# Giving the activations of each large stage an address residue modulo 256 bytes of their own

## The chip, the cores and the metric

The kernel runs as one program on one core of one Trainium2 chip. The metric is the device time of an execution in microseconds, as the median of several runs. Lower is better.

## The reference, cut to what matters

The reference is two stacks of two layers over 256 tokens of 1024 features, all float32. Each layer of the first stack projects the tokens, runs three attentions (latent, differential, memory), mixes them through gates, adds a residual with a layer norm, and runs an MLP of width 4096. Each layer of the second stack projects the tokens to 14,912 columns, runs three scans, mixes them through gates, and runs a gated feed-forward of width 2816.

```python
# first stack, a layer (first_block), cut
x = _layernorm(ALPHA * x + merged @ w_out[l], ln1_g[l], ln1_b[l])
f = jnp.square(jax.nn.relu(x @ mlp_w1[l])) @ mlp_w2[l]
x = _layernorm(ALPHA * x + f, ln2_g[l], ln2_b[l])
...
# second stack, a layer (second_block), cut
u = _rmsnorm(h, norm_mix_g[l])
... = _split(u @ w_in[l], IN_SIZES_2)          # three branches and their gates
h = h + merged @ w_out[l]
u = _rmsnorm(h, norm_ffn_g[l])
up = _dwconv(u @ w_up[l], ffn_conv_w[l], ffn_conv_b[l])
h = h + (jax.nn.silu(a_half) * v_half) @ w_down[l]
```

## The kernel before

**Matrix products.** Weights stream from HBM in 768 panels of 128 partitions x 1024 words. A panel lands in a ring of five (`wring`); ScalarE rounds it to float32r (`whi`), VectorE subtracts to get the rest (`wlo`), in rings of four. Activations are kept in the same two parts in one buffer, a `Pair`: chunks of 256 words, first all high parts, then all low parts 8,192 bytes further on (for the usual 8 chunks). A product is three matmuls: high x high, high x low, low x high.

There are two forms. `features` (built by `projB`) holds the weights (128x128) and moves the activations (128x256): a panel is 2 column halves x 4 chunks x 3 = 24 matmuls. `tokens` (built by `projA`) holds the activations (128x128) and moves the weights (128x512): a panel is 2 token halves x 2 chunks x 3 = 12 matmuls. Both are recorded at line 112, so groups are told apart by their tiles: `ps<-uT,whi` is a `features` matmul on uT, `ps<-whi,uT` a `tokens` one.

**Order.** The schedule is a static list. `weave` interleaves generators with weights, so that panels of a projection fill TensorE between the small matmuls of an attention or scan. Every wait is on a named event; no wait is derived from an address.

**Memory.** `Arena` hands out words of each partition, first fit or at a given place (`at=`), and takes a hole back only five panels after it was freed. It starts at byte 82,496, which is 64 modulo 256. `whi` and `wlo` start at bytes 36,992 and 53,376, both 128 modulo 256, and so does each of their 128x128 blocks. Sizes and places are such that every Pair starts at residue 64 except uT, which lies at word 27,168: byte 191,168, residue 192. The parts inside a Pair are multiples of 256 bytes apart, so each chunk has the residue of its Pair.

**The stages that the change touches**, with the Pair of each:

- first stack, projections of layer 0 and of layer 1: xT, with 34 `features` panels and 24 `tokens` panels per layer; nearly all are woven with attention;
- first stack, MLP of each layer: xT (second one), 32 `features` panels, and hid, 4 times 8 `tokens` panels, in long unbroken runs;
- second stack, projections of each layer ("mix"): uT, 109 `features` and 24 `tokens` panels, woven with the scans in large part; the two scan outputs are written into the same buffer (`uT.again`) for their branch products;
- second stack, up-projection of each layer ("ffn"): uT again, 44 `features` panels without a break.

Pairs that stay as they are, at residue 64: memT, cq, ckv, oM, oD, oE, merged, ym, the 22-chunk hid of the second stack, pT, hT.

Of the kernel before, what the change touches and what calls it, by code (L numbers as in the profile page):

```python
# [9 lines left out]
F32R = mybir.dt.float32r  # L10
# [6 lines left out]
DEPTH = 2  # L17
# [39 lines left out]
class Signals:  # L57
# [5 lines left out]
    def __init__(self, nc, ctx):  # L63
        self.nc, self.ctx = nc, ctx
        self.sems, self.count, self.value, self.sure = {}, {}, {}, False
# [91 lines left out]
class Buf:  # L157
# [1 line left out]


    def __init__(self, name, off, n, ap):
        self.name, self.off, self.n, self.ap = name, off, n, ap

    def again(self, name="again"):

# [28 lines left out]
class Arena:  # L194
# [32 lines left out]
        t = self.nc.alloc_sbuf_tensor_at(name, [128, n], dt, offset=self.base + 4 * o)  # L227
        return kind(name, o, n, t[:, :])

    def pair(self, name, chunks, at=None):  # L230
        return self.take(name, 512 * chunks, F32R, Pair, at=at)

    def give(self, *bufs):
        for b in bufs:
            self.holes.append((b.off, b.n, self.panels))
        self.holes.sort(key=lambda h: h[0])


# [71 lines left out]
def run(g):  # L310
    for _ in g:
        pass
# [89 lines left out]
def schedule(K, a):  # L402

    steps = []
    ar, PB, AB = K.ar, K.PB, K.AB
    panels = []

    def do(kind, *args):
        steps.append((kind, args))
# [61 lines left out]
    def turned(src, n, ready, out, w=128):  # L471

        for c in range(0, n, 2):
            m = min(2, n - c)
            u = AB.take()
            do("turn", u, src, c, m, w, ready)
            out(c, m, u)
            yield

    def to_pair(x):  # L480
        return lambda c, m, u: do("split_bank", x, c, m, u)
# [16 lines left out]
        run(projA(a["mem_w_kv"][l], 512, 512, memT, tokens_to(c.mv, 512)))  # L498
        return c

    xN, memN = ar.take("xN", 2048, at=34272), ar.take("memN", 2048)
    do("load_first", memN)
    xT, memT = ar.pair("xT", 8), ar.pair("memT", 8)
    run(turned(memN.tok(), 8, lambda c, t: ["mem"], to_pair(memT)))
    do("load_second", xN)
    memkv = [mem_kv(0)]
# [11 lines left out]
    def ln_begin(c, res, g, b, tag):  # L518

        n = c.ln = Box()  # L520
        n.tag, n.l, n.g, n.b, n.res = tag, c.l, g, b, res
        n.st = ar.take("lnst", 64, at=25600)
        do("ln_stats", n)
        ar.give(n.st)
        return n
# [13 lines left out]
    def ln_rows(n, gb, xN_):  # L539
        do("ln_rows", n, gb, xN_)  # L540
        ar.give(gb, n.res)
# [6 lines left out]
    def block1(l, xN, xT, later):  # L548
        w = a["w_in"][l]
        c = Box()  # L550
        c.l, c.li = l, float(0.8 - 0.6 * np.exp(-0.3 * l))
        c.small = ar.take("small", 128, top=True)
        sm = c.small.ap
# [178 lines left out]
        run(projA(a["w_out"][l], 0, 1024, merged, out_r(xN, rN, ("ln1", l), lambda t: [("rows", ("ln2", l - 1), t)] if l else ["x"])))  # L732
        ar.give(merged, xN)
        n = ln_begin(c, rN, "ln1_g", "ln1_b", ("ln1", l))
        xT1, xN1 = ar.pair("xT", 8), ar.take("xN", 2048, at=31888)
        ln_features(n, xT1)
        w1, w2 = a["mlp_w1"][l], a["mlp_w2"][l]
        banks = {b0: [PB.take() for _ in range(2)] for b0 in (0, 512)}
# [4 lines left out]
        def out_h(x):  # L743
            def out(k, m, u):
                s = HS.take()
                do("relu_square", x, k, u, s)
                s.freed = (x.name, k)
            return out
        for q in range(5):
            if q < 4:  # L750
                hid = ar.pair("hid", 8)
                run(projB(w1, q * 1024, 1024, xT1, out_h(hid), 0, AB))
                pieces.append(hid)
                if q == 0:
                    ln_rows(n, gb, xN1)
            if q:
                hid = pieces[q - 1]
                run(projA(w2, 0, 1024, hid, None, (q - 1) * 1024, banks=banks, first=q == 1, fin=q == 4))
                ar.give(hid)
# [6 lines left out]
                out(t, b0, 512, banks[b0][t])  # L766
        ar.give(xN1)
        n = ln_begin(c, rN, "ln2_g", "ln2_b", ("ln2", l))
        xT2, xN2 = ar.pair("xT", 8) if l < DEPTH - 1 else None, ar.take("xN", 2048, at=34272)
        if xT2:  # L770
            ln_features(n, xT2)
        return xN2, xT2, lambda: ln_rows(n, gb, xN2)
# [17 lines left out]
    for l in range(DEPTH):  # L790
        xN, xT, later = block1(l, xN, xT, later)
# [4 lines left out]
    def rms_turn(l, g, x, tag):  # L796

        n = Box()
        b = ar.take("rms", 2064, at=6144 if tag[0] == "mix" else 19968)
        n.tag, n.l, n.h, n.ready = tag, l, hN.tok(), list(hkey)  # L800
        n.u3 = b.ap[:, 0:2048].rearrange("p (t f) -> p t f", t=2)
        n.ss, n.rs, n.tmp = b.ap[:, 2048:2050], b.ap[:, 2050:2052], b.ap[:, 2052:2054]
        do("rms_rows", n)
        run(turned(n.u3, 8, lambda c, t: [("rms", tag, t, c // 4)], to_pair_scaled(x, g, l)))
        ar.give(b)

    def block2(l):
        w = a["w_in_2"][l]
        c = Box()
        c.l = l  # L810
        uT = ar.pair("uT", 8, at=27168)
        rms_turn(l, "norm_mix_g_2", uT, ("mix", l))

        def small_gates():
# [82 lines left out]
        C = Box()  # L897
# [15 lines left out]
        def ssd_scan():  # L913
            C.ys, C.X, C.CB = ys, ar.take("sX", 2048, at=20240), ar.take("sCB", 1536, at=15376)
            for k in range(0, 8, 2):
                do("ssd_turn", C, k, AB.take())
                yield
            for g in range(2):
                do("ssd_products", C, g, AB.take())
            ar.give(C.bc)  # L920
            yield
            C.sums = ar.take("ssums", 1280, at=16912)
            C.eslots = [ar.take("sE", 768, at=o) for o in (12304, 13072, 13840, 14608, 24336, 33488)]
            ES, es = Slots(C.eslots), {}
            C.ES = ES

            def exponents(h):
                es[h] = ES.take()
                do("ssd_exponents", c, h, es[h], c.spread[h])
                c.spread[h].freed = [("arg", l, h), ("arg2", l, h)]  # L930

            def decays(h):
                do("ssd_decay", c, h, es[h])
                spread_rows(h + 3)

            def weights(h):
                do("ssd_weights", c, C, h, es[h])

            def outputs(h):
                if h % 2:  # L940
                    u = AB.take()
                    do("ssd_outputs", c, C, h, [es[h - 1], es[h]], u)
                    es[h - 1].freed = es[h].freed = u.full

            def norms(h):
                if h % 8 == 7:
                    do("ssd_norm", c, C, h // 8, AB.take())
            yield from staged(16, (exponents, 0, True), (decays, 1, False), (weights, 2, False), (outputs, 3, False), (norms, 4, True))
            ar.give(C.sums, C.CB)

        M = Box()
# [16 lines left out]
        def ml_scan():  # L968

            M.hb = C.z.again()  # L970
            M.st, M.mvb = ar.take("mst", 192, at=36320), ar.take("mmv", 96, at=36512)
            M.H3 = M.hb.tok()
            M.s6 = M.st.ap[:, 0:96].rearrange("p (t h k) -> p t h k", t=2, h=8)
            M.mv = M.mvb.ap[:, 0:32].rearrange("p (t h k) -> p t h k", t=2, h=8)
            done = ("ys", l, 7)
            ES = Slots(C.eslots, [s.freed for s in C.ES.pieces])
            NS_ = Slots([C.x.part("mN", o, 532) for o in (768, 1300)], [done, done])
            es, us = {}, {}

            def exponents(h):  # L980
                es[h] = ES.take()
                do("ml_exponents", c, h, es[h], c.spread[16 + h])
                c.spread[16 + h].freed = [("arg", l, 16 + h), ("arg2", l, 16 + h)]

            def decays(h):
                us[h] = AB.take()
                do("ml_scores", M, h, us[h])
                do("ml_decay", c, h, es[h])
                spread_rows(16 + h + 3)

            def weights(h):
                do("ml_weights", M, c, h, es[h], us[h])

            def outputs(h):
                e, n = es[h], NS_.take()
                ns = [AB.take(), AB.take()]
                do("ml_outputs", M, c, h, e, n, ns)
                e.freed = ns[1].full
                n.freed = ("mh", l, h)
            yield from staged(8, (exponents, 0, True), (decays, 1, False), (weights, 2, False), (outputs, 3, True))  # L1000
            ar.give(M.k, C.x, *C.eslots)
            yield
            do("ml_norm", M, c)
            ar.give(M.o, M.st, M.mvb)

            M.y = ar.over("ym", M.qv, 4096, F32R, Pair)
            for _ in range(2):
                yield
            yield from turned(M.H3, 8, lambda k, t: [("ml_norm", l, t)], to_pair_scaled(M.y, "ml_norm_g_2", l))
            ar.give(M.hb)  # L1010
# [9 lines left out]
        B0, B1 = Box(), Box()  # L1020
        run(hg_proj(0, B0))
        yh = ar.take("yh", 2048, at=25104)
        c.sm, c.mxb = ar.take("sm", 688, at=31264), ar.take("mxb", 1024, at=31952)
        c.rows = ar.take("rows", 512, at=32976)

        c.spread = {}
        RS = Slots([c.mxb.part("spread", 0, 512), c.mxb.part("spread", 512, 512), c.rows.again("spread")])
# [5 lines left out]
        s, mxb = c.sm.ap, c.mxb.ap  # L1033
# [57 lines left out]
        ar.give(merged)  # L1091
        do("ffn_columns", pr, fc, l, [AB.take(), AB.take()])
        ar.give(pr)
        uT = ar.pair("uT", 8, at=27168)
        rms_turn(l, "norm_ffn_g_2", uT, ("ffn", l))
        hid = ar.pair("hid", 22, at=8192)
        aslots, vslots = [ar.take("fa", 512, at=22032 + 512 * i) for i in range(2)], [ar.take("fv", 512, at=23056 + 512 * i) for i in range(2)]
# [26 lines left out]
        run(projA(a["w_down_2"][l], 0, 1024, hid, add_to_h(("h2", l))))  # L1124
        ar.give(hid)

        pN, pT, ple = ar.take("pN", 512, at=33312), ar.pair("pT", 2, at=24576), ar.take("ple", 2048, at=31264)
        do("load_ple", pN, l, len(panels) - 1)
        run(turned(pN.tok(256), 2, lambda k, t: [("ple", l)], to_pair(pT)))
        ar.give(pN)  # L1130
# [1502 lines left out]
```

How the kernel before makes its waits and increments, by code:

```python
    def then_inc(self, sem, by=1):  # L96
        return self
# [8 lines left out]
    def wait_ge(self, sem, n):  # L106
        if self.e is not None and self.seen.get(id(sem), 0) < n:
            self.e.wait_ge(sem, n)
            self.seen[id(sem)] = n
# [1060 lines left out]
    def bank_free(u):  # L1170
        if u.before:
            e.wait_ge(*at(u.before))
# [1 line left out]
    def tokens(p, x, us, q0, first, fin):  # L1174
        e.wait_ge(*at(("lo", p.i)))
        for t in range(2):
            o = us[t].ap[:, 0:p.nb]
            if first:
                bank_free(us[t])
            for k in range(p.nk):
                e.wait_ge(*at((x.name, q0 + k)))
                xh, xl = x.at(q0 + k, t * 128, 128)
                e.matmul(o, xh, p.hi[:, k, :], start=first and k == 0, stop=False)
                e.matmul(o, xh, p.lo[:, k, :], start=False, stop=False)
                m = e.matmul(o, xl, p.hi[:, k, :], start=False, stop=fin and k == p.nk - 1)
            m.then_inc(*up("pe_panel", ("panel", p.i, t)))
# [1 line left out]
    def features(p, x, u, q0, chunks):  # L1188
        e.wait_ge(*at(("lo", p.i)))
        if q0 == 0:
            bank_free(u)
        for j0 in range(0, p.nb, 128):
            w = min(128, p.nb - j0)
            o = u.ap[0:w, 2 * j0:2 * j0 + 256]
            for k in range(p.nk):
                q = q0 + k
                e.wait_ge(*at((x.name, q)))
                xh, xl = x.at(q)
                ch, cl = p.hi[:, k, j0:j0 + w], p.lo[:, k, j0:j0 + w]
                e.matmul(o, ch, xh, start=q == 0 and j0 == 0, stop=False, skip_group_check=True)
```

## Time and profile before

| | us |
|---|---|
| median of 3 runs (lowest to highest) | 2776.11 (2772.51 to 2781.39) |
| the profiled execution, its own time | 2774.6 |
| span of the profiled execution | 2772.8 |
| TensorE busy in the span | 2552.8 |
| VectorE busy | 1814.9 |
| ScalarE busy | 1432.1 |

The span runs from the first to the last instruction of the profiled execution; 1.8 us lie around it. TensorE's busy time is the union of its matmuls, which overlap each other: one matmul of 128x256 lasts some 280 ns in the records while the next one starts some 115 ns after it. What counts for time is the distance between starts, called the pitch below.

### The profile page before, as it was taken

What the parts mean: (1) busy time and instruction counts of PE and PEld (TensorE: products, weight loads), DVE (VectorE), ACT (ScalarE), POOL (GpSimd) and SP (SyncE); (2) the same over time, 40 slices, a digit from 0 to 9 for tenths busy, and PEclk for the clock granted to TensorE, in tenths of its full rate; (3) what the DMA queues carried; (4) which work ended last, traced back from release to release, by engine and by line L of the source; (5) the groups of instructions that cost most, each with busy time, mean ns of one, the idle gap of its engine ahead of it and who ended that gap; (6) DMA issues with size and microseconds to landing.
All of it is one profiled execution on the core that took longest, in us unless ns stands there. A gap on an engine that the chain in (4) does not pass through costs nothing.

```text
span 2772.8 us, 42179 instructions
## 1 busy us (share of the span) xinstructions
PE 2552.8 (92%) x17296; PEld 2334.2 (84%) x17296; DVE 1814.9 (65%) x2912; ACT 1432.1 (52%) x2077; POOL 211.0 (8%) x187
## 2 busy tenths in 40 slices
PE   8998999999999997978999889998978999889997
PEld 7887989878889896977997888996978997888986
DVE  4556676565667655567677776864567677676864
ACT  4546545454564543555555435654555555435653
POOL 0000000000000000000116100000000116200000
PEclk9999999999999998989999999999989999999998
DMA  6553456655435565533566535654533566535663
GB/s 224 160 145 92 145 176 190 197 157 149 119 103 189 166 194 170 149 84 107 143 183 174 148 125 162 188 195 150 148 85 107 149 180 170 156 122 167 184 194 106
DMA packets 358670, 426.24 MB, mean 154 GB/s; under 512 B 21176, under 2 KB 286862, under 8 KB 358478
## 3 DMA queue, kind: packets, MB, share of 16 engines
q1 hardware_dynamic: 342602, 401.95, 48.2%
q10 hardware_dynamic: 14068, 15.91, 2.5%
q0 software_dynamic: 1808, 5.69, 0.6%
q8 instruction: 137, 2.24, 0.3%
q14 instruction: 55, 0.45, 0.0%
HBM read 422.35 MB, written 1.15 MB: 153 GB/s over the span
## 4 chain that ended last, share of the span: by engine, by line
PE 69%; DVE 17%; ACT 8%; issue 4%; DMA 1%; POOL 0%; ACTq 0%; DVEq 0%; POOLq 0%
PE ps L112 66%; DVE wlo L121 4%; ACT whi L118 3%; PE ps L115 2%; DVE sE L121 2%; ACT hgKm L118 1%; DVE hgA L148 1%; ACT E L118 1%; DVE hgQF L121 1%; DVE hgQB L121 1%; ACT L118 1%; DVE xN L121 1%; DVE E L124 1%; DVE hgkb L121 1%; DVE hgkf L121 1%
## 5 line engine op out<-in xcount | busy, mean ns | idle before, releaser
L121 DVE TENSOR_TENSOR wlo<-wring,whi 128x1024 fp32r<-128x1024 f32 x768 | 929.3, 1219 | 596.1 <-ACT whi L118 595.3
L118 ACT ACTIVATE whi<-wring 128x1024 fp32r<-128x1024 f32 x768 | 802.0, 1052 | 454.3 <-PE ps L112 445.0
L112 PE MATMUL ps<-uT,whi 128*128 128x256 f32 x4896 | 900.8, 286 | 27.7 <-DVE uT L121 27.7
L112 PEld LDWEIGHTS ps<-uT,whi 128*128 128x128 f32 x4896 | 768.0, 192 | 34.3 <-issue 33.3
L112 PE MATMUL ps<-uT,wlo 128*128 128x256 f32 (+1 forms) x2448 | 694.0, 284 | 0.0
L112 PEld LDWEIGHTS ps<-uT,wlo 128*128 128x128 f32 (+1 forms) x2448 | 469.5, 192 | 0.0
L112 PE MATMUL ps<-xT,whi 128*128 128x256 f32 x2112 | 382.0, 285 | 0.6 <-DVE wlo L121 0.6
L112 PEld LDWEIGHTS ps<-xT,whi 128*128 128x128 f32 x2112 | 327.4, 191 | 6.7 <-issue 3.3
L112 PE MATMUL ps<-xT,wlo 128*128 128x256 f32 x1056 | 296.8, 281 | 0.0
L112 PE MATMUL ps<-whi,hid 128*128 128x512 f32 x864 | 268.7, 391 | 0.0
L112 PEld LDWEIGHTS ps<-xT,wlo 128*128 128x128 f32 x1056 | 201.2, 191 | 0.1
L112 PEld LDWEIGHTS ps<-whi,hid 128*128 128x128 f32 x864 | 162.3, 188 | 35.1
L112 PE MATMUL ps<-wlo,hid 128*128 128x512 f32 x432 | 169.7, 393 | 0.0
L112 PE MATMUL ps<-whi,xT 128*128 128x512 f32 x384 | 132.3, 406 | 0.0
L112 PE MATMUL ps<-whi,uT 128*128 128x512 f32 x384 | 129.3, 408 | 0.0
L124 POOL TENSOR_SCALAR sE<-mxb,sm 128x256 f32<-128x256 f32 x64 | 98.4, 1547 | 259.0 <-DMA mxb<-spread 247.0
L118 ACT ACTIVATE E<-ps,E 128x256 f32<-128x256 f32 x112 | 52.2, 473 | 119.1 <-DVE E L124 118.9
L112 PE MATMUL ps<-hgQm,hgKm 128*128 128x128 f32 x448 | 69.9, 320 | 38.0 <-ACT hgKm L118 31.1
L118 ACT ACT_TABLE_LOAD x77 | 98.8, 1283 | 3.3 <-issue 1.8
L112 PEld LDWEIGHTS ps<-hgQm,hgKm 128*128 128x128 f32 x448 | 65.4, 231 | 40.8 <-ACT hgKm L118 32.7
L112 PEld LDWEIGHTS ps<-wlo,hid 128*128 128x128 f32 x432 | 81.1, 188 | 17.5
L118 ACT ACTIVATE hgQm<-hgQF 128x512 f32<-128x512 f32 x28 | 17.9, 641 | 139.1 <-DVE hgTb L121 120.6
(372 smaller groups left out, 3530.5 us busy)
## 6 DMA issues: line engine op xcount, KB each, us to landing
wring<-in_w_in SPq DMA_DIRECT2D x346, 512.0 KB, 4.0
wring<-in_mlp_w SPq DMA_DIRECT2D x128, 512.0 KB, 4.3
wring<-in_w_up SPq DMA_DIRECT2D x88, 512.0 KB, 4.4
wring<-in_w_down SPq DMA_DIRECT2D x44, 512.0 KB, 4.5
wring<-in_w_branch SPq DMA_DIRECT2D x32, 512.0 KB, 3.5
wring<-in_w_out SPq DMA_DIRECT2D x32, 512.0 KB, 4.0
wring<-in_mem_w_kv SPq DMA_DIRECT2D x16, 512.0 KB, 5.2
mxb<-spread ACTq DMA_DIRECT2D x32, 256.0 KB, 5.7
```

The source lines that it names most:

```text
L112: return self.e.matmul(*p, **k) if self.e else Nothing()
L115: return self.e.transpose(*p, **k) if self.e else Nothing()
L118: return self.e.activation(*p, **k) if self.e else Nothing()
L121: return self.e.tensor_tensor(*p, **k) if self.e else Nothing()
L124: return self.e.tensor_scalar(*p, **k) if self.e else Nothing()
L148: return self.e.copy_predicated(*p, **k) if self.e else Nothing()
```

## The change

`Arena.pair` gets a parameter `skew`, in words. It takes 64 words more and places the Pair `skew` words into them; `hold` remembers the larger piece, so that `give` returns all of it. Since 64 words are 256 bytes, the residue of such a Pair is that of its piece plus four times the skew.

| stage | Pair | residue before | skew | residue after |
|---|---|---|---|---|
| first stack, projections, layer 0 | xT | 64 | 16 | 128 |
| MLP layer 0 | xT | 64 | 8 | 96 |
| MLP layer 0, quarters 0 to 3 | hid | 64 | 16, 8, 24, 4 | 128, 96, 160, 80 |
| first stack, projections, layer 1 | xT | 64 | 24 | 160 |
| MLP layer 1 | xT | 64 | 4 | 80 |
| MLP layer 1, quarters 0 to 3 | hid | 64 | 56, 40, 1, 12 | 32, 224, 68, 112 |
| mix, layer 0 and 1 | uT | 192 | 56, 40 | 32, 224 |
| ffn, layer 0 and 1 | uT | 192 | 16, 1 | 128, 68 |

```diff
-    def pair(self, name, chunks, at=None):
-        return self.take(name, 512 * chunks, F32R, Pair, at=at)
+    def pair(self, name, chunks, at=None, skew=None):
+        if skew is None:
+            return self.take(name, 512 * chunks, F32R, Pair, at=at)
+        hold = self.take(name, 512 * chunks + 64, F32R, Pair, at=at)
+        p = Pair(hold.name, hold.off + skew, 512 * chunks, hold.ap[:, skew:skew + 512 * chunks])
+        p.hold = hold
+        return p
...
-    xT, memT = ar.pair("xT", 8), ar.pair("memT", 8)
+    xT, memT = ar.pair("xT", 8, skew=16), ar.pair("memT", 8)
...
-        xT1, xN1 = ar.pair("xT", 8), ar.take("xN", 2048, at=31888)
+        xT1, xN1 = ar.pair("xT", 8, skew=(8, 4)[l]), ar.take("xN", 2048, at=31888)
...
-                hid = ar.pair("hid", 8)
+                hid = ar.pair("hid", 8, skew=((16, 8, 24, 4), (56, 40, 1, 12))[l][q])
...
-        xT2, xN2 = ar.pair("xT", 8) if l < DEPTH - 1 else None, ar.take("xN", 2048, at=34272)
+        xT2, xN2 = ar.pair("xT", 8, skew=24) if l < DEPTH - 1 else None, ar.take("xN", 2048, at=34368)
...
-        b = ar.take("rms", 2064, at=6144 if tag[0] == "mix" else 19968)
+        b = ar.take("rms", 2064, at=(15488, 6144)[l] if tag[0] == "mix" else 19968)
...
-        uT = ar.pair("uT", 8, at=27168)
+        uT = ar.pair("uT", 8, at=27200, skew=(56, 40)[l])
...
-            M.st, M.mvb = ar.take("mst", 192, at=36320), ar.take("mmv", 96, at=36512)
+            M.st, M.mvb = ar.take("mst", 96, at=36416), ar.take("mmv", 96, at=36512)
...
-        uT = ar.pair("uT", 8, at=27168)
+        uT = ar.pair("uT", 8, at=27200, skew=(16, 1)[l])
```

To make room, xN moves by 96 words (residue 192 to 64), and so do the small buffers above uT: sm, mxb, rows, one of the six sE slots, pN and ple, each 96 words higher; `rms` of the mix in layer 0 moves to word 15,488. No instruction is added or removed, no shape changes, and no event or wait changes.

## Rows read from the trace of the kernel before

**Rows 1.** The page, busy time by engine and the chain that ended last.

```profile
PE 2552.8 (92%) x17296; PEld 2334.2 (84%) x17296; DVE 1814.9 (65%) x2912; ACT 1432.1 (52%) x2077; POOL 211.0 (8%) x187
...
PE ps L112 66%; DVE wlo L121 4%; ACT whi L118 3%; PE ps L115 2%; DVE sE L121 2%; ACT hgKm L118 1%; DVE hgA L148 1%; ACT E L118 1%; DVE hgQF L121 1%; DVE hgQB L121 1%; ACT L118 1%; DVE xN L121 1%; DVE E L124 1%; DVE hgkb L121 1%; DVE hgkf L121 1%
```

**Rows 2.** The page, costliest TensorE group: busy, mean ns | idle before.

```profile
L112 PE MATMUL ps<-uT,whi 128*128 128x256 f32 x4896 | 900.8, 286 | 27.7 <-DVE uT L121 27.7
```

**Rows 3.** Windows of TensorE (length, busy, count, clock, DMA): MLP, mix, ffn.

```profile
401.00:441.00 40.00, 39.70 (x351) 1.00 0.59 184
...
1111.80:1656.00 544.20, 490.66 (x3519) 0.94 0.49 139
1708.50:1833.00 124.50, 124.50 (x1057) 1.00 0.57 178
```

**Rows 4.** Windows, matmuls with tile uT: inside the ffn stage, layer 0.

```profile
1712.00:1832.00 120.00, 120.00 (x1021) 1.00 0.59 185
```

**Rows 5.** Windows, matmuls with tile xT: inside the MLP, layer 0.

```profile
466.00:485.00 19.00, 19.00 (x170) 1.00 0.56 183
```

**Rows 6.** Windows, matmuls with tile ym: branch product right after uT.

```profile
1657.00:1677.00 20.00, 20.00 (x179) 1.00 0.55 184
```

**Rows 7.** Windows, matmuls with tile hid: `tokens` panels at residue 64.

```profile
1834.00:1892.00 58.00, 58.00 (x255) 1.00 0.62 199
```

**Rows 8.** Timeline of TensorE: `tokens` panels on uT, first and last.

```profile
1502.96 0.39 PE L112 MATMUL ps<-wlo,uT 128*128 128x512 f32 x1
...
1509.26 0.40 PE L112 MATMUL ps<-wlo,uT 128*128 128x512 f32 x1
```

**Rows 9.** Timeline of TensorE: xT at residue 64, two panels either side of a stop.

```profile
286.21 0.39 PE L112 MATMUL ps<-xT,whi 128*128 128x256 f32 x2
...
287.91 0.39 PE L112 MATMUL ps<-xT,whi 128*128 128x256 f32 x2
...
290.29 0.40 PE L112 MATMUL ps<-xT,whi 128*128 128x256 f32 x2
...
293.47 0.40 PE L112 MATMUL ps<-xT,whi 128*128 128x256 f32 x2
```

**Rows 10.** Timeline of TensorE: uT at residue 192, two panels either side of a stop.

```profile
1547.65 0.40 PE L112 MATMUL ps<-uT,whi 128*128 128x256 f32 x2
...
1549.77 0.40 PE L112 MATMUL ps<-uT,whi 128*128 128x256 f32 x2
...
1553.07 0.39 PE L112 MATMUL ps<-uT,whi 128*128 128x256 f32 x2
...
1557.83 0.39 PE L112 MATMUL ps<-uT,whi 128*128 128x256 f32 x2
```

**Rows 11.** Groups of TensorE between 1108 and 1700 us.

```profile
L112 PE MATMUL ps<-ym,whi 128*128 128x256 f32 x128 | 21.8, 276 | 0.0
...
L112 PE MATMUL ps<-mqv,sE 128*128 128x129 f32 x96 | 12.7, 280 | 5.7 <-DVE sE L121 5.4
L112 PE MATMUL ps<-mqv,mk 128*128 128x256 f32 x32 | 8.2, 378 | 0.0
...
L112 PE MATMUL ps<-hgq,hgKm 128*128 128x128 f32 x32 | 4.1, 281 | 2.2 <-DVE hgKm L121 2.2
```

**Rows 12.** Waits of TensorE between 1108 and 1700 us, longest first.

```profile
PE ps L112 <- ACT hgKm L118: 15.9, 5, 6.0
PE ps L112 <- DVE uT L121: 13.8, 2, 9.5
```

**Rows 13.** Instructions that write or read uT: VectorE's writes of the low parts.

```profile
L121 DVE TENSOR_TENSOR uT<-ys,uT x8: 658/682/687, 1586.0 to 2417.1; 128x512 fp32r<-128x512 f32 x8
```

**Rows 14.** Costliest groups of the whole trace: VectorE's writes into hid.

```profile
L121 DVE TENSOR_TENSOR hid<-relu,hid 128x512 fp32r<-128x512 f32 x32 | 22.2, 692 | 1.1
```

**Rows 15.** Timeline of TensorE: the seam from uT to ym.

```profile
1656.08 0.28 PE L112 MATMUL ps<-uT,wlo 128*128 128x256 f32 x1
1656.20 0.40 PE L112 MATMUL ps<-ym,whi 128*128 128x256 f32 x2
```

More of the change, by code:

```diff
@@ L161, in __init__ @@
     def __init__(self, name, off, n, ap):
-        self.name, self.off, self.n, self.ap = name, off, n, ap
+        self.name, self.off, self.n, self.ap, self.hold = name, off, n, ap, None
     def again(self, name="again"):
@@ L228, in piece @@
         return kind(name, o, n, t[:, :])
-    def pair(self, name, chunks, at=None):
-        return self.take(name, 512 * chunks, F32R, Pair, at=at)
+    def pair(self, name, chunks, at=None, skew=None):
[5 more added lines that the diff above has]
+        return p
     def give(self, *bufs):
         for b in bufs:
-            self.holes.append((b.off, b.n, self.panels))
+            h = b.hold or b
+            self.holes.append((h.off, h.n, self.panels))
         self.holes.sort(key=lambda h: h[0])
@@ L499, in mem_kv @@
         return c
-    xN, memN = ar.take("xN", 2048, at=34272), ar.take("memN", 2048)
+    xN, memN = ar.take("xN", 2048, at=34368), ar.take("memN", 2048)
     do("load_first", memN)
-    xT, memT = ar.pair("xT", 8), ar.pair("memT", 8)
+    xT, memT = ar.pair("xT", 8, skew=16), ar.pair("memT", 8)
     run(turned(memN.tok(), 8, lambda c, t: ["mem"], to_pair(memT)))
@@ L922, in ssd_scan @@
             C.sums = ar.take("ssums", 1280, at=16912)
-            C.eslots = [ar.take("sE", 768, at=o) for o in (12304, 13072, 13840, 14608, 24336, 33488)]
+            C.eslots = [ar.take("sE", 768, at=o) for o in (12304, 13072, 13840, 14608, 24336, 33584)]
             ES, es = Slots(C.eslots), {}
@@ L1022, in block2 @@
         yh = ar.take("yh", 2048, at=25104)
-        c.sm, c.mxb = ar.take("sm", 688, at=31264), ar.take("mxb", 1024, at=31952)
-        c.rows = ar.take("rows", 512, at=32976)
+        c.sm, c.mxb = ar.take("sm", 688, at=31360), ar.take("mxb", 1024, at=32048)
+        c.rows = ar.take("rows", 512, at=33072)
         c.spread = {}
@@ L1125, in block2 @@
         ar.give(hid)
-        pN, pT, ple = ar.take("pN", 512, at=33312), ar.pair("pT", 2, at=24576), ar.take("ple", 2048, at=31264)
+        pN, pT, ple = ar.take("pN", 512, at=33408), ar.pair("pT", 2, at=24576), ar.take("ple", 2048, at=31360)
         do("load_ple", pN, l, len(panels) - 1)
```

## The prediction, made before the changed kernel was run

> **What bounds the kernel now.** I read the page first. TensorE is busy 92% of the span, and the chain that ended last lies 69% on it, nearly all in the helper line of the matmuls [rows 1]. The costliest TensorE groups are the matmuls on uT [rows 2]. So the next question is what sets the pace there: a wait, or the matmuls themselves. The windows by stage answer it. In the ffn stage TensorE is busy in all of 124.5 us, in the MLP in 39.70 of 40, at the full granted clock in both (1.00, the 2.4 GHz level); in the mix stage 53.5 of 544.2 us are idle [rows 3], and the longest waits there are for the scan's operands (15.9 us) and for uT itself (13.8 us) [rows 12]. In the runs without a break only the pitch of the matmuls counts.
>
> The pitch is the quantity to read for this change. A window counts every matmul that touches it, the one already under way too, so pitch = (window + 0.28 us) / count. For `features` matmuls:
>
> - uT, residue 192, ffn: 120.28/1021 = 117.8 ns [rows 4]; the other layer's window gives the same
> - xT, residue 64, MLP: 19.28/170 = 113.4 ns [rows 5]
> - ym, residue 64, the branch product after uT: 20.28/179 = 113.3 ns [rows 6]
>
> For `tokens` matmuls, which last 0.39 us: hid at 64, (58+0.39)/255 = 229.0 ns [rows 7]; uT at 192, 27 matmuls from 1502.96 to 1509.26 us, 233.3 ns [rows 8]. So there is a fast and a slow pitch, 4.5 ns and 4.3 ns apart, and uT has the slow one whether it is moved or held.
>
> The residue is not the whole of it. In one buffer at 64 the pitch is 113.3 ns (15 matmuls from 286.21 to 287.91) before a stop and 117.8 ns (27 from 290.29 to 293.47) after it [rows 9]. In uT at 192 it is 117.8 ns (18 from 1547.65) and after a stop 113.3 ns (42 from 1553.07) [rows 10]. TensorE holds a pitch until something interrupts it, and the restart picks one. Counted panel by panel from such start times: in the `features` panels on xT in the first stack's projections that follow a stop the two pitches come 25 times each; in the mix stages 66 of 70 restarts on uT take the slow one. All 88 ffn panels and 48 `tokens` panels of uT are slow, and 195 of its 218 mix `features` panels; all 64 MLP panels of xT, all 64 of hid and all 16 of ym are fast. That is a large difference between buffers, and the residue is the difference that I know of. The other is the place: uT alone lies above byte 191,000.
>
> **The change, part by part.**
>
> *No instruction is added.* The matmuls, evictions and DMAs are the same in number, shape and order. Moved buffers (xN, sm, mxb, rows, sE, pN, ple, rms) cost nothing in themselves: VectorE's 128x512 writes into uT at 192 take 682 ns and those into hid at 64 take 692 ns [rows 13, 14], 10 ns apart, in an engine that is idle a third of the span [rows 1].
>
> *Price of a pitch.* A `features` panel is 24 x 4.5 = 108 ns, a `tokens` panel 12 x 4.3 = 52 ns.
>
> *What a new residue does* no row shows: only 64 and 192 occur. Bounds from these two: each stage could have the behaviour of 64 or of 192. I take for each stage the nearer one on the circle of 256: 32, 68, 80, 96 and 112 behave as 64; 160 and 224 as 192; 128 is as far from both, and is taken at half.
>
> Gains:
> - mix, layer 0 (192 to 32): 100 slow panels. Unbroken panels become fast, those after a stop half the time, so I let three quarters of them go: 75 x 108 = 8.1 us, and 24 x 52 = 1.2 us. TensorE is busy 90% of this stage, and part of what it gains it then waits for the scan, whose chain doesn't shorten: 85% of it counts, 7.9 us. In the layer 1 mix (224) nothing.
> - ffn, layer 1 (192 to 68): 44 x 108 = 4.8 us, all of it, as nothing else ever holds TensorE up there [rows 3].
> - ffn, layer 0 (192 to 128): half, 2.4 us.
> Sum 15.1 us.
>
> Losses:
> - projections of the first stack, layer 0 (64 to 128): 18 fast `features` and 23 fast `tokens` panels, 1.9 + 1.2 us, half of it: 1.6 us. Layer 1 (64 to 160): 18 and 21, 1.9 + 1.1 = 3.0 us.
> - hid: a quarter is 8 panels, 0.42 us; those at 160 and 224 in full, that at 128 by half: 1.0 us.
> - MLP xT (96 and 80): nothing.
> Sum 5.6 us.
>
> *The start of four bytes.* Skew 1 (residue 68) is the only one that is no multiple of 16 bytes; it serves ffn layer 1 (1,056 moving reads) and one quarter of hid. A row speaks for no cost: V is moved in blocks of 129 words that start at 129 times the head's number, so at every residue modulo 16, and its matmuls last 280 ns against 281 for the evenly placed 128-column ones [rows 11]. But that is plain float32, which takes twice the time per column: 378 ns for 256 columns against 276 in float32r [rows 11]. If a float32r read off its pair fell back to that rate, it would cost 1,056 x 102 ns = 108 us. Bounds 0 and 108 us; I take 0, being nearest to the row that has such starts.
> The Trainium skill speaks of this under "SBUF — State Buffer", section "Specifications (TRN2)": SBUF is read in 16-byte lines and each crossing to a new line pays. By it a moving row of 1,024 bytes at residue 68 touches 65 lines in place of 64, an estimate of some 1.6% or 2 us for this ffn stage, and all other new residues would be worth nothing, so the time would be 2 us above before. The two pitches in one buffer and the uT difference already go beyond that rule, so I give it a part of the chance of "no change" below only.
>
> *Sum.* Own time 2774.6 - 15.1 + 5.6 = 2765.1 us. The profiled execution is 1.5 us (0.05%) below the median of 2776.1, so the median should be 2776.1 - 9.5 = 2766.6, say **2767 us**.
>
> **The rivals.**
>
> *64 is the rule and 192 the exception.* Then uT goes fast everywhere and nothing is lost: 2 x 7.9 + 2 x 4.8 = 25 us, **2751 us**. For it: 64 is fast both as moving and as held operand. Against: one good residue out of two says little of eleven.
>
> *Not the residue but the place or the neighbours.* uT stays above byte 191,000 and the scans around it remain. Then nothing moves: **2776 us**. For it: both pitches occur at both residues [rows 9, 10]. Against: the pitch turns from 117.8 to 113.3 at the seam from uT to ym with no stop (the last matmul on uT starts at 1656.08, the first on ym at 1656.20 [rows 15]; the pitches are in [rows 6, 10]), although the surroundings are the same; that leaves the place.
>
> *Slower: 64 is the exception.* If nearly all other residues are slow as 192 is, uT gains nothing and the first stack loses: MLP 64 x 108 = 6.9 us, hid 64 x 52 = 3.3 us, projections 36 x 108 + 44 x 52 = 6.2 us; sum 16.4 us, **2792 us**. For it: the activations at 64 are the only fast ones seen. It decides against the forecast as soon as 32 and 68 are slow: the gain is then 2.4 us or less against a loss of 5.6 or more.
>
> *Slower: the four-byte start costs a pass.* Up to 108 us, **2870 us**, in one stage alone. It decides from about 10 ns per matmul on.
>
> **How the numbers follow.** Chances: forecast case 0.42, 64 the rule 0.19, place or no effect 0.18, 64 the exception 0.16, the four-byte start 0.05. Within the forecast case each stage can fall either way; a wrong guess for 32 costs 8 us, for 68 5 us, a lucky one for 224 gives 8, so its own range is 2757 to 2776. Below 2748 lie the best tenth, above 2791 half of "the exception" and the four-byte case: the range of 8 in 10 is 2748 to 2791. Faster by over 0.3% (8.3 us, about what this measurement can tell from no change) means below 2767.8: 0.27 of the forecast case and all of "the rule", 0.46. Slower by over 0.3%: the two slower rivals, 0.21. Within: 0.33.
>
> **What the changed profile would show.** The window of ffn layer 1 (uT at 68) should hold matmuls 113.3 ns apart, as should unbroken panels of mix layer 0 (uT at 32); mix layer 1 (uT at 224) should stay at 117.8, and xT in the projections of layer 1 (at 160) should restart slow nearly always. MLP windows (96, 80) should stay at 113.3. The ffn of layer 0 says what 128 does. The forecast is wrong if uT stays at 117.8 at 32 and 68 (then place, or the exception), if the MLP leaves 113.3, or if a third pitch appears, above all at 68 or at 128, where activations and weights have one residue.

## The result and the profile after

| | before | changed |
|---|---|---|
| median, us (4 runs each) | 2774.31 (2769.76 to 2781.39) | 2790.93 (2788.65 to 2796.28) |
| ratio | | 1.006, 95% interval 1.0033 to 1.0088 |
| span of the profiled execution, us | 2772.8 | 2786.8 |

The change makes the kernel slower by 0.6%, some 17 us. The forecast was 9 us faster. The time is near the rival "64 is the exception" (2792 us).

The page of the changed kernel answers to [rows 1, 2]. The chain has the same shape; TensorE is busy 16.5 us longer for the same 17,296 matmuls, and the wait in front of uT is the same 27.7 us:

```profile
PE 2569.3 (92%) x17296; PEld 2349.7 (84%) x17296; DVE 1812.5 (65%) x2912; ACT 1431.6 (51%) x2077; POOL 212.6 (8%) x187
...
L112 PE MATMUL ps<-uT,whi 128*128 128x256 f32 x4896 | 911.8, 288 | 27.7 <-DVE uT L121 27.7
```

So no wait was added: the time outside TensorE's busy time is 220.0 us before and 217.5 after. The matmuls themselves are further apart. Windows of the changed kernel, matmuls on xT (MLP of layer 0 at residue 96, of layer 1 at 80); columns: window, length, busy time and count, granted clock, DMA share, GB/s. They answer to [rows 5]:

```profile
467.00:486.00 19.00, 19.00 (x163) 1.00 0.58 190
926.00:946.00 20.00, 20.00 (x170) 1.00 0.58 167
```

The same view of uT: ffn of layer 0 (128), ffn of layer 1 (68), unbroken panels of the mix at 32 and at 224. They answer to [rows 4]:

```profile
1720.00:1840.00 120.00, 120.00 (x1002) 1.00 0.60 184
2552.00:2672.00 120.00, 120.00 (x989) 1.00 0.59 178
1130.00:1157.00 27.00, 27.00 (x232) 1.00 0.65 178
1960.00:1985.00 25.00, 25.00 (x211) 1.00 0.65 178
```

With pitch = (window + 0.28 us)/count as before, these are 118.3 and 119.3 ns on xT (113.4 before), and 120.0, 121.6, 117.6 and 119.8 ns on uT (117.8 before). The granted clock is 1.00 in all of them, so the clock has no part in these pitches. None of the residues in these windows reaches 113.3.

Nor is it the other engines' writes: in the ffn of layer 0 the trace has the starts of three matmuls in a row 360 ns apart in all 274 cases with ScalarE or VectorE writing new weights meanwhile, and in 75 of 77 cases with neither writing. In the kernel before it is 353 or 354 ns either way. (The transfers that land new weights were not told apart in this way.)

All of TensorE by stage in the changed kernel: MLP 0, MLP 1, mix 0, ffn 0, mix 1, ffn 1, to the start of what follows. They answer to [rows 3]:

```profile
397.60:588.00 190.40, 183.62 (x1168) 0.98 0.58 179
922.00:1123.60 201.60, 185.53 (x1170) 0.96 0.57 173
1123.60:1663.00 539.40, 486.94 (x3518) 0.95 0.50 140
1716.00:1842.00 126.00, 126.00 (x1052) 1.00 0.57 176
1954.00:2496.20 542.20, 489.88 (x3518) 0.96 0.50 140
2549.00:2677.00 128.00, 128.00 (x1054) 1.00 0.57 173
```

The same view of the kernel before, of MLP 0, MLP 1 and ffn 1:

```profile
397.10:583.80 186.70, 179.58 (x1169) 0.98 0.59 183
915.70:1111.80 196.10, 179.73 (x1169) 0.95 0.58 177
...
2537.90:2662.60 124.70, 124.70 (x1058) 1.00 0.57 178
```

From start to start of their first panels the MLPs grew from 186.7 and 196.1 us to 190.7 and 201.4, the ffn stages from 124.7 each to 126.8 and 128.6: 15.3 us together, more than the 14.0 us by which the spans differ. The two mixes, where matmuls on uT are 2,904 of some 3,520, did not grow (544.4 and 543.8 before, 539.7 and 542.6 now), although layer 1's pitch rose from 117.8 to 120.0. The stretches from the first panel of the projections to the MLP grew by 0.9 us (layer 0) and 1.8 us (layer 1). That the stages without a break grew and the mixes did not is followed up below.

### The profile page after: what moved, and what is told of

The parts are those of the page before. It is cut to its first block, busy times and chain, and to the rows that moved or that the text cites. A ratio compares the mean times of both kernels' runs of the same rounds, so it can differ in the third digit from the quotient of the medians.

```text
span 2786.8 us, 42179 instructions
## 1 busy us (share of the span) xinstructions
PE 2569.3 (92%) x17296; PEld 2349.7 (84%) x17296; DVE 1812.5 (65%) x2912; ACT 1431.6 (51%) x2077; POOL 212.6 (8%) x187
## 4 chain that ended last, share of the span: by engine, by line
PE 69%; DVE 17%; ACT 8%; issue 4%; DMA 1%; POOL 0%; ACTq 0%; DVEq 0%; POOLq 0%
PE ps L112 67%; DVE wlo L121 4%; ACT whi L118 3%; PE ps L115 2%; DVE sE L121 2%; ACT hgKm L118 1%; DVE hgA L148 1%; ACT E L118 1%; DVE hgQF L121 1%; DVE hgQB L121 1%; ACT L118 1%; DVE E L124 1%; DVE hgkf L121 1%; DVE hgkb L121 1%; DVE ys L130 1%
## 5 line engine op out<-in xcount | busy, mean ns | idle before, releaser
L112 PE MATMUL ps<-uT,whi 128*128 128x256 f32 x4896 | 911.8, 288 | 27.7 <-DVE uT L121 27.7
L112 PE MATMUL ps<-xT,whi 128*128 128x256 f32 x2112 | 393.6, 289 | 0.0
```

Of the source, the lines that this page charges most:

```text
L112: return self.e.matmul(*p, **k) if self.e else Nothing()
```

## The experiments

The kernel before ran beside each set; each ratio is to those runs. In the later runs, edits are given against the changed kernel where they only set skews.

**Places only** (`e1_places_only`): is it the residues, or the moved buffers?

```diff
-    xT, memT = ar.pair("xT", 8, skew=16), ar.pair("memT", 8)
+    xT, memT = ar.pair("xT", 8, skew=0), ar.pair("memT", 8)
... (skew 0 for every xT and hid)
-        uT = ar.pair("uT", 8, at=27200, skew=(56, 40)[l])
+        uT = ar.pair("uT", 8, at=27200, skew=(32, 32)[l])
... (and for the ffn)
```

> The changed kernel with every buffer where the change puts it (the larger pieces, uT's piece at word 27,200, xN, sm, mxb, rows, sE, pN, ple and rms moved), but with the residues of before: skew 0 for xT and hid (64), skew 32 for uT (192). Theory R (the residues of the Pairs alone make the change's time): same as the kernel before, 2774 us within 0.3%; uT 117.8 ns per features matmul in the ffn stages, xT 113.3 in the MLP. Rival P (the moved places and neighbours make it): some or all of the 16.6 us remain, up to 2791 us, with pitches above those of before.

Measured: 2771.30 us against 2771.51, ratio 1.0003 (0.9991 to 1.0015). The pitches are those of before; uT in the ffn of layer 0:

```profile
1710.00:1825.00 115.00, 115.00 (x979) 1.00 0.61 184
```

That is 117.8 ns. The moved places cost nothing that can be seen (the interval allows 4 us): rival P falls, and the residues make the change's time.

**All at 64** (`e2_all_64`): the same kernel with skew 0 for uT too.

> As the run before this one, but with skew 0 for uT too, so that every Pair of the kernel starts at residue 64. Theory R: uT takes the fast pitch of the other buffers, 113.3 ns in both ffn stages and in the unbroken panels of the mix, tokens panels on uT 228.9 in place of 233.3; 25 us less than before by the terms of the prediction (2 x 7.9 + 2 x 4.8), about 2749 us. Rival P (uT is slow for its place at the top of the partition, not for its residue): uT stays at 117.8 ns and the time at 2774 us.

Measured: 2761.25 us, ratio 0.997 (0.9954 to 0.9987), 8 us faster by the ratio (the medians are 10 us apart). uT in the ffn stages of layer 0 and 1:

```profile
1712.00:1824.00 112.00, 112.00 (x990) 1.00 0.62 190
2532.00:2645.00 113.00, 113.00 (x999) 1.00 0.62 192
```

113.4 ns in both. uT is not slow for its place at the top of the partition. The size was off by a factor of three: of 109 `features` panels per mix only 50 and 62 took the fast pitch, since restarts at 64 pick either, and the time gained is less than the pitches gave up, as the last run takes up. A part of it went to the clock. In the 24 runs of the kernel before in this set the time falls as the mean granted clock rises, from 2777.02 us at 0.958 to 2764.32 us at 0.964, some 1.7 us for each 0.001; the seven runs here had 0.957 on average, those 24 had 0.9605. That is an estimate of 6 us given back.

**Weights at 0** (`e3_weights_0`): distance or the activations' own residue? The constants are 2,208 words, so `whi` and `wlo` move up by 8,832 bytes, which is 128 modulo 256; no other buffer changes its residue.

```diff
-    K.whi, K.wlo = sb("whi", NS * WN, F32R), sb("wlo", NS * WN, F32R)
     cst = K.cst = sb("cst", C_END)
+    K.whi, K.wlo = sb("whi", NS * WN, F32R), sb("wlo", NS * WN, F32R)
```

> The kernel before, with the constants allocated ahead of the two weight rings in place of behind them: whi and wlo start at residue 0 in place of 128, and nothing else changes its residue. Theory D (what counts is the distance between the residues of the operand that moves and of the one that is loaded): uT at 192 is now as far from the weights as 64 was (64 - 128 = 192 - 0 modulo 256), so the ffn stages go from 117.8 to 113.3 ns, and xT at 64 as far as 192 was, so the MLP goes from 113.3 to 117.8 ns; the time falls by about 25 us for uT and rises by about 16 for the first stack, some 9 us below before, and ym and hid turn slow too. Theory A (only the residue at which the activations themselves start counts): nothing changes, 117.8 on uT, 113.3 on xT, 2774 us.

Measured: 2775.85 us, ratio 1.0015 (1.0001 to 1.0028). No activation moved, and yet xT in the MLP, ym, and the 22-chunk hid, one window each in this order, left their pitches:

```profile
406.00:430.00 24.00, 24.00 (x206) 1.00 0.60 175
...
1663.00:1682.00 19.00, 19.00 (x164) 1.00 0.57 180
...
1842.00:1898.00 56.00, 56.00 (x242) 1.00 0.61 194
```

They are 117.9 and 117.6 ns against 113.3, and (56+0.39)/242 = 233.0 ns against 229.0 [rows 5, 6, 7]. On uT the `tokens` panels went the other way: 42 of 48 at 228.8 (none before), and 143 of 218 mix `features` panels at 113.3 (9 before). Theory A falls. The forecast of 9 us less missed, and the trace shows a part of why: the swap was not complete. Both ffn stages on uT stayed at 117.8 ns, start to end, which leaves out 9.6 of the 25 us forecast for uT. At either distance a `features` train (matmuls without a break) can lock into 113.3 or 117.8; the distance sets which one it tends to find.

**A map** (`e4_map`, `e6_map2`): other skews in the same lists, one profile each.

```diff
# e4_map: xT 52 and 20 (projections), (48, 60) (MLP); uT (36, 44) (mix), (28, 2) (ffn)
+                hid = ar.pair("hid", 8, skew=((48, 52, 60, 2), (20, 28, 36, 44))[l][q])
# e6_map2: xT 44 and 12 (projections), (44, 16) (MLP); uT (16, 46) (mix), (44, 8) (ffn)
+                hid = ar.pair("hid", 8, skew=((10, 13, 14, 15), (17, 18, 20, 22))[l][q])
```

> The changed kernel with eleven other residues, to read more points of the map from one profile. Moved activations: first-stack projections 16 and 144, MLP xT 0 and 48, mix 208 and 240, ffn 176 and 72. Held activations in hid: 0, 16, 48, 72 and 144, 176, 208, 240. If the pitch follows the residue smoothly, 48 and 72 come out near the 113.3 ns of 64, and 176 between the 116.7 of 160 and the 117.8 of 192. If 64 is one isolated point, as 80 (118.9) and 68 (121.7) suggest, 48 and 72 are near 118 and above. If a start that is no multiple of 16 bytes costs a fixed part, 72 is slow as 68 was, and 48 and all the others are below 120.1. By the mean of the pitches so far, 118 ns, about 2790 us.

> More points of the map in one look. Moved: 240 in the first-stack projections of layer 0, the MLP of layer 0 and the ffn of layer 0; 112 in the projections and 128 in the MLP of layer 1; mix 128 and 248; ffn 96 in layer 1. Held in hid: 104, 116, 120, 124 and 132, 136, 144, 152. If the residue sets the pitch wherever it is used: 240 gives 113.3 in all three kinds of stage, 128 gives 120.0 in the MLP and in the mix, 96 gives 118.2 in the ffn. If the stage sets it, 240 is fast in the mix alone. Held: if the 226.7 ns of 128 is the floor of a valley from 112 (228.5) on, the values between lie between; if it is one point, 124 and 132 are above 230.

Measured: 2787.4 and 2783.0 us, one run each. The pitch of a panel is taken as the mean distance of the starts in its second half, and the table has the median over a stage's panels, all at the 2.4 GHz level, from the profiles of before, changed and these two; weights at 128. "Moved" are activations in `features` panels, "held" those in `tokens` panels:

| residue | moved, ns | held, ns | | residue | moved, ns | held, ns |
|---|---|---|---|---|---|---|
| 0 | 118.8 | 232.6 | | 120, 124 | | 233.3, 226.7 |
| 16 | 118.5, some 116.7 | 233.0 | | 128 | 120.0 | 226.7 |
| 32 | 117.5 | 233.3 | | 132, 136 | | 232.4, 230.6 |
| 48 | 119.4 | 229.2 | | 144, 152 | 116.7 or 118.5 to 118.8 (144) | 233.3, 230.0 |
| 64 | 113.3 or 117.8 | 228.8 | | 160 | 116.7 | 233.3 |
| 68, 72 | 121.7, 120.0 | 233.5, 230.5 | | 176 | 118.3 | 233.3 |
| 80 | 118.9 | 231.7 | | 192 | 117.8, rarely 113.3 | 233.3 |
| 96 | 118.2 | 233.7 | | 208 | 120.0, some 118.3 | 232.2 |
| 104, 112 | 117.2 (112) | 231.2, 228.5 | | 224 | 120.0 | 234.3 |
| 116 | | 233.3 | | 240, 248 | 113.3, 122.1 | 233.3, 226.7 |

Where two values stand in one cell with a comma they belong to the two residues in order. 64 and 192 are not the only ones with two pitches: at 208 80 of the mix's panels are at 120.0 and 23 at 118.3, at 144 14 are at 116.7 and 15 at 118.5 to 118.8. Nothing here is smooth: 64 lies between 119.4 and 121.7, 240 between 120.0 and 122.1. The residue sets the pitch wherever it is used: 240 is fast in a mix, in an MLP (31 of 32 panels) and in the ffn (43 of 44), 128 is 120.0 in four stages, 96 is 118.2 in an MLP and an ffn. uT in the ffn of layer 0 at 240, from the second map:

```profile
1720.00:1834.00 114.00, 114.00 (x1008) 1.00 0.62 191
```

113.4 ns. In a mix 94 of 109 `features` panels at 240 are at 113.3, where 64 had 50 and 62: its restarts find the fast pitch.

**The changed kernel with weights at 0** (`e7_after_w0`), the same two-line edit as above.

> The changed kernel with the weight rings at residue 0 in place of 128, as in the earlier run on the kernel before. Theory D (the distance counts) takes every stage's pitch from the map at its residue plus 128: MLP of layer 0 (96) as 224, 120.0 ns in place of 118.2; MLP of layer 1 (80) as 208, 118 to 120; ffn of layer 0 (128) as 0, 118.7 in place of 120.0; mix 32 as 160, 116.7, and 224 as 96, 118.2 in place of 120.0; held: 128 as 0, 232.4 in place of 226.7, 112 as 240, 233.3 in place of 228.5. Theory A (the activations' own residue counts) keeps the pitches of the changed kernel in all of them.

Measured: 2799.8 us, one run. xT in the MLPs (96 and 80), uT in the ffn stages (128 and 68):

```profile
470.00:489.00 19.00, 19.00 (x161) 1.00 0.56 185
930.00:950.00 20.00, 20.00 (x169) 1.00 0.55 158
...
1730.00:1850.00 120.00, 120.00 (x1014) 1.00 0.60 184
2564.00:2684.00 120.00, 120.00 (x1020) 1.00 0.59 183
```

Medians by panel: 120.0 at 96 (the map at 224: 120.0), 120.0 at 80 (at 208: 120.0), 118.8 at 128 (at 0: 118.8), held 128 at 233.3 (at 0: 232.6), held 80 at 232.2 (at 208: 232.2), held 112 at 233.3 (at 240: 233.3). The mix at 224 reads 118.3 (at 96: 118.2). Theory D had named all but the held 80 beforehand. In one place it is half right: the mix at 32 should have read 116.7 and reads 117.8 in 57 panels and 116.7 in 46. Residue 160 with weights at 128 has the same two: in the profile of the first half alone (below) 23 panels on xT are at 116.7 and 7 at 117.8. The last window is the start of four bytes: 68 costs 121.7 ns against weights at 128 and 117.9 against weights at 0. By its distance it stands where 196 would with weights at 128, and next to that the map has 192, at 117.8. So no price of such a start by itself can be seen.

**One half of the change each** (`e8_first_only`, `e11_second_only`).

```diff
# e8: the changed kernel, uT at its old residue in mix and ffn
+        uT = ar.pair("uT", 8, at=27200, skew=(32, 32)[l])
# e11: the changed kernel, skew 0 for every xT and hid
```

> The change in the first stack only: xT and hid with their new residues, uT at 192 as before, all buffers in the changed kernel's places. In the changed kernel's trace the first matmul on uT starts 12.5 us later than before, and the rest of the span is 1.5 us longer. If the stages add up, this run is 12 to 13 us above before, 2784 us, ratio 1.0045. If losing uT's pitches in the second stack is the larger part (the mix at 224 at 120.0, the ffn at 121.7), it is nearer to 2775 us.

> The change in the second stack only: uT at 32 and 224 in the mixes and at 128 and 68 in the ffn stages, xT and hid at 64 as before. The first-stack half of the change alone measured 1.0049. If the halves add up to the 1.006 of the whole change, this one is at 1.001, 2 to 4 us above before. By pitches: mix 32 nothing, mix 224 103 panels x 53 ns = 5.4 us, ffn 128 44 x 53 = 2.3 us, ffn 68 44 x 94 = 4.1 us, together up to 12 us, which would be 1.004.

Measured: first stack alone 2785.25 us, ratio 1.0049 (1.0032 to 1.0065), 13.6 us by the ratio; second stack alone 2780.50 us, ratio 1.0026 (1.0015 to 1.0037), 7 us. Both are real, and together they agree with the whole within the intervals. The second lies between the 1.001 and the 1.004 of its expectation; in its profile the two ffn stages are 2.1 and 3.9 us longer than before and the mixes no longer. The first stack, where the good residue was given up, is the larger part.

**Residues chosen by the map** (`e5_chosen`, `e9_240_128`).

```diff
# e5, against the changed kernel; e9 has 44 (residue 240) in place of 0 too
-    xT, memT = ar.pair("xT", 8, skew=16), ar.pair("memT", 8)
+    xT, memT = ar.pair("xT", 8, skew=44), ar.pair("memT", 8)
-        xT1, xN1 = ar.pair("xT", 8, skew=(8, 4)[l]), ar.take("xN", 2048, at=31888)
+        xT1, xN1 = ar.pair("xT", 8, skew=(0, 0)[l]), ar.take("xN", 2048, at=31888)
...
+                hid = ar.pair("hid", 8, skew=((16, 16, 16, 16), (16, 16, 16, 16))[l][q])
...
+        uT = ar.pair("uT", 8, at=27200, skew=(44, 44)[l])
...
+        uT = ar.pair("uT", 8, at=27200, skew=(0, 0)[l])
-        hid = ar.pair("hid", 22, at=8192)
+        hid = ar.pair("hid", 22, at=8192, skew=16)
```

> Residues chosen from the pitches read so far: 240 where moved activations are woven with other work (first-stack projections, both mixes), since uT at 240 had 113.3 ns in 94 of its 109 panels of a mix, against 50 and 62 at residue 64; 64 in the unbroken stages (both MLPs, both ffn); 128 for held activations (the eight hid quarters and the 22-chunk hid), which had 226.7 ns against 228.8. By the sum of pitches, from the 2761.3 us of all-64: mixes 72 more fast panels x 108 ns less 48 tokens panels x 53 ns, at 85%: 4.4 us; hid 108 panels x 25 ns: 2.7 us; first-stack projections 31 x 108 less 44 x 53 ns: 1.0 us. About 2753 us, ratio 0.993 or 0.994. If the basin a restart takes depends on the neighbours more than on the residue, the mix gains nothing and the time is 2759 to 2762 us.

> As the chosen residues of the run at 2750.5 us, but with 240 in place of 64 for the moved activations of the MLPs and the ffn stages too, since at 64 the second and third MLP quarter had fallen to 117.8 ns after a hid at 128, and one of the two ffn stages stayed at 117.8 ns from its start on, while 240 gave 113.3 in 31 of 32 MLP and 43 of 44 ffn panels. If 240 has one pitch however it is entered: 32 MLP and 44 ffn panels x 108 ns less, 8 us, about 2743 us where the run at 2750.5 had one slow ffn stage, ratio to before 0.990 to 0.991. If the sequence of stages decides and not the residue, some of them turn slow again and it is no faster than that run, 0.993.

Measured: 2750.54 us against 2769.94, ratio 0.993 (0.9917 to 0.9944), as expected; and 2751.84 against 2772.51, ratio 0.9922 (0.9905 to 0.9938), not the 2743 hoped for. The two cannot be told apart. Both beat the kernel before and the changed one. The first met its number, not all its terms: 76 panels at 64 in the unbroken stages were at 117.8 ns, some 8 us that the forecast did not have, and the mixes gained 8 us on all at 64 by the profiles, where it had 4.4. All of TensorE in its two mixes, and the 22-chunk hid at 128, held:

```profile
1112.00:1648.20 536.20, 478.89 (x3521) 0.95 0.50 141
1934.00:2470.00 536.00, 479.28 (x3521) 0.95 0.50 141
...
1826.00:1881.00 55.00, 55.00 (x244) 1.00 0.65 201
```

The mixes took 1072.2 us against 1088.2 in the profile of before, and hid (55+0.39)/244 = 227.0 ns against 229.0. The first run also shows how a train at 64 is caught in the wrong pitch. The timeline of TensorE in it, at the seam from a hid at 128 (held) to xT at 64:

```profile
462.68 0.39 PE L112 MATMUL ps<-whi,hid 128*128 128x512 f32 x1
462.90 0.40 PE L112 MATMUL ps<-xT,whi 128*128 128x256 f32 x2
463.14 0.28 PE L112 MATMUL ps<-xT,wlo 128*128 128x256 f32 x1
463.26 0.40 PE L112 MATMUL ps<-xT,whi 128*128 128x256 f32 x2
...
464.32 0.40 PE L112 MATMUL ps<-xT,whi 128*128 128x256 f32 x2
```

Twelve matmuls from 462.90 to 464.32 are 118.3 ns apart; the eight panels there stay at 117.8 to their end, where the same xT at 64 was at 113.3 in the 16 panels ahead of the first hid. The two quarters of xT that follow a hid at 128 are slow in both layers, 32 panels of 32; after a hid at 64 none is, in the profiles of before, places only and all at 64. And one ffn stage at 64 locked slow for all 44 panels, the other fast:

```profile
1703.00:1823.00 120.00, 120.00 (x1021) 1.00 0.61 184
2525.00:2639.00 114.00, 114.00 (x1009) 1.00 0.62 189
```

117.8 and 113.3 ns. With 240 in the second of these kernels, MLPs and ffn were all at 113.3 but for the first panels; its ffn of layer 0:

```profile
1705.00:1820.00 115.00, 115.00 (x1017) 1.00 0.62 192
```

In its profile that ffn stage took 120.4 us against 124.8, and the MLPs 1.0 and 1.3 us less; projections and mixes were 0.9 to 1.7 us longer each. The profile has some 24 us more in stretches at the 1.2 GHz level (mean granted clock 0.959 against 0.963), and over all runs the mean clock was 0.959 against 0.961.

**Only wlo at 0** (`e10_wlo_0`).

```diff
-    K.whi, K.wlo = sb("whi", NS * WN, F32R), sb("wlo", NS * WN, F32R)
+    K.whi = sb("whi", NS * WN, F32R)
     cst = K.cst = sb("cst", C_END)
+    K.wlo = sb("wlo", NS * WN, F32R)
```

> The kernel before with the constants allocated between whi and wlo: whi stays at residue 128, wlo goes to 0. If the distance counts matmul by matmul (the block that is loaded while another operand streams), xT in the MLP and ym, two thirds of whose matmuls use whi, have 113.3, 113.3 and 117.8 ns, mean 114.8, uT mostly 117.8, 117.8 and 113.3, mean 116.3, and hid (228.9 x 2 + 233.3)/3 = 230.3. If the whole train locks to one pitch, a stage is at 113.3 or 117.8, and with both blocks at different distances most likely at 117.8.

Measured: 2772.6 us, one run (before 2772.5). uT in an ffn stage and xT in an MLP:

```profile
1710.00:1828.00 118.00, 118.00 (x995) 1.00 0.59 183
...
400.00:424.00 24.00, 24.00 (x214) 1.00 0.58 171
```

118.9 ns on uT and 113.5 on xT: neither theory. Held operands read 230.5 on average, near what matmul by matmul gave (230.3), though single panels lie between 228.5 and 231.7. Moved ones do not average: 64 stayed at 113.3, and did so in 62 of 68 projection panels too, with no slow pitch in any, where both pitches came before; and uT had 113.3 in 86 mix panels, 118.9 in nearly all others. The pitch can't be put together from those of single pairs of operands; that it belongs to the sequence of three is a reading of this one run.

**Only the mixes at 224** (`e12_mix_224`): what does a woven stage make of a slower pitch?

```diff
# the places-only kernel, with one line changed
+        uT = ar.pair("uT", 8, at=27200, skew=(40, 40)[l])
```

> Residues of before in every Pair but uT in the two mixes, which goes from 192 to 224, the slowest residue seen there (120.0 ns for features, 234.4 for tokens). Nothing else differs in time: ffn at 192, first stack at 64. If the woven stages turn pitch into time as the prediction took it (85%), each mix loses about 100 panels x 53 ns + 24 x 13 ns = 5.6 us, together 9.6 us, ratio 1.0035. If they absorb it, since a slower train leaves TensorE less idle and fewer stretches at the 1.2 GHz level (in the changed kernel's profile mix layer 1 took 542.6 us in place of 543.8 with pitches worth 6.7 us more), the ratio is within 0.999 and 1.0015.

Measured: 2773.91 us against 2770.95, ratio 1.0014 (1.0 to 1.0028), the second of the two cases. All `features` panels of both mixes but a few were at 120.0. But in the profiled run the ffn of layer 0 on uT at 192 had locked fast this time, which no earlier run with 192 there had (first row; layer 1 at 117.7 below it):

```profile
1713.00:1827.00 114.00, 114.00 (x1008) 1.00 0.61 190
2539.00:2657.00 118.00, 118.00 (x1005) 1.00 0.59 182
```

In the profiled run that is worth 5 us; what this stage did in the other eleven no trace shows, so the whole run's time may hide a part of the loss. The mixes of this run and of the places-only run, all of TensorE:

```profile
1114.60:1658.60 544.00, 493.42 (x3521) 0.95 0.49 139
1941.80:2484.70 542.90, 491.13 (x3520) 0.95 0.49 140
```

```profile
1112.70:1653.00 540.30, 484.58 (x3520) 0.96 0.51 140
1940.60:2482.40 541.80, 489.35 (x3518) 0.94 0.51 139
```

1086.9 against 1082.1 us: 4.8 us for pitches worth some 13 us, where the prediction's 85% would make 11. Against the profile of before (1088.2 us) it is nothing, and the two profiles with uT at 192 lie 6 us apart. Taken over all profiles with weights at 128, a mix lasts 542.6 us on average at 192 (six mixes, 540.3 to 544.4), 542.8 at 224 (four, 541.6 to 544.0) and 537.4 at 240 (five, 535.9 to 540.7). So 6 us of slower pitch per mix cost nothing that these profiles show, and 10 us of faster pitch bring about half. Why stays open. A slower train may leave fewer stretches at the 1.2 GHz level: those sum to some 204 us in the changed kernel's profile and 244 in that of before, but one profile of each is no proof.

## Why the prediction was wrong, point by point

- *That the residue matters, by way of the pitch of the matmuls* was right: with the residues put back the time is back (1.0003), and the changed kernel has the same waits and a longer matmul train.
- *The step that failed* is "I take for each stage the nearer one on the circle of 256: 32, 68, 80, 96 and 112 behave as 64". Moved, none of them did: 117.5, 121.7, 118.9, 118.2 and 117.2 ns. As held operand 112 did (228.5), the others not. The function has narrow dips, at 64 and 240 for moved and at 48, 64, 112, 124 to 128 and 248 for held operands among the points tried. Two points were no ground for an interpolation. The sign that the prediction had named for this, a third pitch and an MLP that leaves 113.3, is what came.
- *Gains.* Mix layer 0: forecast 7.9 us, its `features` pitch went from 117.8 to 117.5, and its `tokens` pitch stayed at 233.3. (The stage was 4.7 us shorter, but so it was, by 4.1, with uT still at 192 in the places-only run.) ffn layer 1: forecast 4.8 us less, measured 3.9 more (68). ffn layer 0: forecast 2.4 less, measured 2.1 more (128). I had allowed only the two pitches I knew, and there are others above 117.8.
- *Losses.* The MLPs, with xT costed at nothing and hid at 1.0 us, gave 9.3 of the 15.3 us. The projections, costed at 4.6 us, gave 2.7. The hid quarter at 128, costed as a loss, gained (226.7 against 228.8).
- *The start of four bytes* taken at 0: right as to the start itself as far as the run with other weights shows (117.9 ns), but 68 was the slowest stage of all with the weights at 128. The two bounds of 0 and 108 us were far apart where the answer was 9 us in pitches against the hoped 113.3.
- *The rival "64 is the exception"* was right in kind and hit the number partly by luck: it had 16.4 us in the first stack, which measured 13.6 alone, and nothing in the second, which measured 7 alone.
- *The rival of place* fell with the first run. *"64 is the rule"* fell with the map. As a size, its 25 us for uT at 64 measured 8: half of the mix panels stayed slow, 85% of pitch turned into time was too much for a woven stage, and the granted clock was lower.
- *Role.* The prediction took one residue for both forms. The map has them apart: 128 is among the best held and the worst moved, 240 among the best moved and slow held.
- *What sets the pitch.* Shown: the distance between the residues of activations and weights, since moving the weights by 128 bytes modulo 256 moved the pitches of operands that lay still, and to those that the map has at the same distance. At distances 64 and 192 (modulo 256) it sets which of two pitches is likely, not which one comes. The Trainium skill, "TensorE: Matmul & The Clock Gate", section "Part 2: What happens when you issue a matmul", says that the moving operand and the weight load have independent read ports and that loading the next weights takes no SBUF read bandwidth from the running matmul. Read strictly, weights at 0 would then have changed nothing; hid went from 229.0 to 233.0 ns. The measurement decides here: the pitch depends on both addresses together. That the two reads disturb each other is the near reading, and by what means was not shown; no run here takes one of the two reads away.
- *What stays open*: why the dips are where they are, why a `features` train can hold either of two pitches at one residue until the next interruption, and why a mix turns so little of a pitch into time.

## What to carry to other kernels

Read the pitch of the matmuls (window and count, or start to start) stage by stage before treating a busy TensorE as at its peak: here the same matmul ran 113.3 to 122.1 ns apart by nothing but the addresses of its operands. Address residues are a parameter to measure, for moved and held operands separately, against the weights' own residue, with every stage of one profiled run carrying another value; do not interpolate between two of them. Gains in unbroken stages come through nearly in full (an ffn stage of 1,056 matmuls went from 124.7 to 120.6 us for 4.4 ns less each), gains in woven ones by about half, and losses there hardly. Look at the granted clock of all runs too: it can give back a part.

## What the hardware showed that was not expected

- float32r matmuls of 256 columns ran at 19 residues between 113.3 and 122.1 ns apart, those of 512 columns with a held operand between 226.7 and 234.3.
- The pitch depends on the residue modulo 256 bytes of activations relative to weights, and can change within four bytes: held, 120 gives 233.3 and 124 gives 226.7 ns.
- A train can be bistable: at 64 both 113.3 and 117.8 ns were held over tens of panels, with the choice made at a restart or at a seam.
- New residues alone took 19 to 21 us off the kernel: ratios 0.993 (0.9917 to 0.9944) and 0.9922 (0.9905 to 0.9938), with the same instructions.
